# Four of 22 row pieces of the indexer's sum on GpSimd in place of VectorE

## What is computed

```python
isc = jax.nn.relu(jnp.einsum('bqhd,bsd->bqhs', qib, k_idx).astype(jnp.float32))
isc = jnp.einsum('bqh,bqhs->bqs', wib.astype(jnp.float32), isc) * idx_scale
isc = jnp.where(admissible[None], isc, -jnp.inf)
top_val, top_idx = lax.top_k(isc, top_k)
```

## Time and profile before

| | us |
|---|---|
| median of 3 runs | 3939.31 (3933.16 to 3941.74) |
| profiled execution, its own time | 3942.32 |
| its span, first to last instruction | 3940.5 |
| VectorE's additions of the indexer, L2115 and L2118 | from 1899.96 to the end of the stage |

### The profile page before, as it was taken

How to read it: one execution, slowest core, us unless ns; L and a number is a source line. 1 busy time by engine, 2 the same in 40 slices (tenths; PEclk the granted TensorE clock), 3 DMA queues, 4 the chain that set the end, 5 groups by cost and what they waited for, 6 DMA issues and landing times. The chain is left out here.

```text
span 3940.5 us, 83555 instructions
## 1 busy us (share of the span) xinstructions
PE 3586.9 (91%) x32524; PEld 3086.8 (78%) x32524; DVE 2307.3 (59%) x5832; ACT 2064.4 (52%) x4636; POOL 766.7 (19%) x657
## 2 busy tenths in 40 slices
PE   5999999889899989979679989976899999999899
PEld 4777899878687768867557987965688888888687
DVE  6100110057898973320699989977677777777322
ACT  4222111156788862212677657554577777777311
POOL 3222100012666640002005425314100000000000
PEclk9999999989999999989899999988899999999899
DMA  5333321196442323452313354235744443341432
GB/s 192 108 117 112 122 81 49 52 204 156 98 97 64 79 74 132 142 197 98 87 43 123 117 168 139 92 135 197 170 96 90 98 92 87 85 97 45 148 122 79
DMA packets 332879, 441.66 MB, mean 112 GB/s; under 512 B 17608, under 2 KB 254792, under 8 KB 322760
## 3 DMA queue, kind: packets, MB, share of 16 engines
q1 hardware_dynamic: 250328, 318.54, 30.6%
q10 hardware_dynamic: 82176, 117.98, 8.1%
HBM read 272.37 MB, written 164.10 MB: 111 GB/s over the span
## 5 line engine op out<-in xcount | busy, mean ns | idle before, releaser
L1265 PEld LDWEIGHTS s_o<-s_v,s_pT 128*64 128x64 f32 x13056 | 402.2, 138 | 89.7 <-issue 68.9
L1265 PE MATMUL s_o<-s_v,s_pT 128*64 128x64 f32 x13056 | 436.9, 224 | 20.3 <-issue 20.3
L211 PE MATMUL s_acc<-s_wh,s_hT 128*128 128x256 f32 (+1 forms) x1408 | 430.5, 306 | 7.1 <-ACT s_parts L624 3.1
L212 PE MATMUL s_acc<-s_wl,s_hT 128*128 128x256 f32 (+1 forms) x1408 | 429.4, 305 | 0.0
L213 PE MATMUL s_acc<-s_wh,s_hT 128*128 128x256 f32 (+1 forms) x1408 | 429.1, 305 | 0.0
L1418 ACT ACTIVATE s_probs<-s_probs,s_nmx 128x512 f32<-128x512 f32 (+3 forms) x640 | 417.0, 657 | 11.7 <-DVE s_nmx L1464 11.7
L211 PE MATMUL s_acc<-s_hT,s_wh 128*128 128x512 f32 x880 | 351.4, 399 | 67.4 <-DVE s_wl L310 29.7
L1250 PE MATMUL s_s<-s_kh,s_qs 128*128 128x512 f32 (+3 forms) x944 | 376.1, 402 | 32.5 <-ACT s_pos L2099 12.3
L1453 DVE CUSTOM_DVE_ANT_0 s_probs<-s_s,s_scores 128x512 f32<-128x512 f32 (+3 forms) x640 | 371.3, 607 | 7.8 <-PEq L91 7.6
L2191 DVE TENSOR_SCALAR_CACHE_REDUCE s_scratch<-s_scores,s_thr 128x384 uint8<-128x384 f32 (+4 forms) x320 | 365.3, 1209 | 1.1
L212 PE MATMUL s_acc<-s_hT,s_wh 128*128 128x512 f32 x880 | 348.6, 396 | 0.0
(11 more groups left out here) (248 smaller groups left out, 7751.1 us busy)
## 6 DMA issues: line engine op xcount, KB each, us to landing
fm<-s_parts ACTq DMA_DIRECT2D x120, 512.0 KB, 2.8
s_qs<-fm SPq DMA_DIRECT2D x60, 512.0 KB, 6.5
y<-s_g SPq DMA_DIRECT2D x20, 1024.0 KB, 5.1
s_y<-y SPq DMA_DIRECT2D x32, 640.0 KB, 6.1
kc<-s_parts ACTq DMA_DIRECT2D x32, 512.0 KB, 2.9
s_kh<-kc SPq DMA_DIRECT2D x30, 512.0 KB, 10.3
s_kl<-kc SPq DMA_DIRECT2D x30, 512.0 KB, 11.9
s_w<-in_o_fm SPq DMA_DIRECT2D x25, 512.0 KB, 4.7
```

Source lines behind the costliest of these rows:

```text
L211: nc.tensor.matmul(out, sh, mh, start=(j == 0), stop=False)
L212: nc.tensor.matmul(out, sh, ml, start=False, stop=False)
L1265: last = nc.tensor.matmul(o_ps[r:r + HD, 0:HD], pT[:, x * P + r:x * P + r + HD], v[:, g.u.kbs[g.a + x], vc:vc + HD], start=(g.first and x ...
```

## The change

Of each head's 22 pieces four, (4,0) of 640 columns, (10,8) of 384, (12,8) of 640 and (14,8) of 896, go to GpSimd. In head 0 GpSimd multiplies such a piece into the sums by one `tensor_scalar`. In heads 1 to 7 it takes two instructions: `tensor_scalar` weighs the piece in place in `pos`, and, behind a wait for that one (`weighed`), `tensor_tensor` adds it to the sums. `added` is now two semaphores, one for each adder, and ScalarE waits for the one of the engine that holds the buffer. TensorE's and ScalarE's work, the order of the units and the rings stay.

```diff
+    BY_POOL = ((4, 0), (10, PB), (12, PB), (14, PB))
     units = [(h, b, a, m) for h in range(I_HEADS) for b, a, m in pieces]
+    adder = ["p" if (b, a) in BY_POOL else "v" for _, b, a, _ in units]
+    nth = [adder[:ui + 1].count(adder[ui]) for ui in range(len(units))]
...
-        added = sc.sem("added")
+        added = {"v": sc.sem("added_v"), "p": sc.sem("added_p")}
+        weighed = sc.sem("weighed")
...
                     if ui >= 4:
-                        act.wait_ge(added, ui - 3)
+                        act.wait_ge(added[adder[ui - 4]], nth[ui - 4])
...
                 for ui, (h, b, a, m) in enumerate(units):
+                    if adder[ui] == "p":
+                        continue
...
                     else:
-                        dve.wait_ge(added, ui - per_head + 1)
+                        dve.wait_ge(added["v"], nth[ui - per_head])
...
+            @block.gpsimd
+            def _(pool):
+                pool.wait_ge(w_made, 1)
+                for ui, (h, b, a, m) in enumerate(units):
+                    if adder[ui] == "v":
+                        continue
+                    dst, src = scores(b)[:, a * P:(a + m) * P], pos[ui % 4][:, 0:m * P]
+                    pool.wait_ge(clipped, ui + 1)
+                    if h == 0:
+                        nc.gpsimd.tensor_scalar(dst, src, w[:, b, h:h + 1], None, ALU.mult).then_inc(added["p"], 1)
+                    else:
+                        pool.wait_ge(added["p"], nth[ui - per_head])
+                        nc.gpsimd.tensor_scalar(src, src, w[:, b, h:h + 1], None, ALU.mult).then_inc(weighed, 1)
+                        pool.wait_ge(weighed, nth[ui] - len(BY_POOL))
+                        nc.gpsimd.tensor_tensor(dst, dst, src, ALU.add).then_inc(added["p"], 1)
```

More of the change, by code:

```diff
@@ L2114, in _ @@
                     if h == 0:
-                        nc.vector.tensor_scalar(dst, src, w[:, b, h:h + 1], None, ALU.mult).then_inc(added, 1)
+                        nc.vector.tensor_scalar(dst, src, w[:, b, h:h + 1], None, ALU.mult).then_inc(added["v"], 1)
                     else:
-                        dve.wait_ge(added, ui - per_head + 1)
+                        dve.wait_ge(added["v"], nth[ui - per_head])
                         nc.vector.scalar_tensor_tensor(out=dst, in0=src, scalar=w[:, b, h:h + 1], in1=dst,
-                                                       op0=ALU.mult, op1=ALU.add).then_inc(added, 1)
+                                                       op0=ALU.mult, op1=ALU.add).then_inc(added["v"], 1)
+            @block.gpsimd
[13 more added lines that the diff above has]
+                        nc.gpsimd.tensor_tensor(dst, dst, src, ALU.add).then_inc(added["p"], 1)
 class Search:
```

## The result

| | median | runs |
|---|---|---|
| before | 3939.4 us | 4, 3933.2 to 3941.7 |
| changed | 3967.6 us | 4, 3965.6 to 3968.2 |

The ratio is 1.0081 (1.0069 to 1.0094): 28 us by the medians, 32 by the ratio, 27 to 37 by its interval. The prediction said 3968, range 3953 to 3988, slower.

The account below looks back on a forecast made before the run. VectorE was taken to bound heads 1 to 7 at 20.6 us each. GpSimd's holds of 7.35 us less 3.2 saved gave +4.1 a head, 28.9 on 3939.3, so 3968 us, range 3953 to 3988.

Parts of the forecast that it names:

- The bound: In heads 1 to 7 VectorE sets the pace, 20.6 us a head without idle time; the other engines wait for it.
- What is taken: Four pieces' additions leave VectorE in each of heads 1 to 7, 3.2 us a head; VectorE alone would need 17.4.
- `tensor_tensor`, 6.24 us a head: GpSimd's four additions in each of heads 1 to 7, at 2.18 ns a column and 0.165 us fixed.
- `tensor_scalar`, 2.87 us a head at the `CAST`'s rate: GpSimd's four weighings in each of heads 1 to 7, at 0.84 ns a column and 0.18 us fixed; upper bound 6.24.
- Turns, one instruction at a time, whichever came first goes first: VectorE and GpSimd alternate when both read SBUF; each GpSimd instruction costs VectorE its duration less some 0.22 us.
- The holds, 7.35 us a head: Time GpSimd's eight instructions keep VectorE waiting in each of heads 1 to 7: 9.11 us less 1.8.
- The ring, 0 to 14 us, taken as 0: ScalarE waiting for buffers of GpSimd's slower pieces: at most 0.5 us for each of 28 pieces, expected just in time.
- The sum, +28.9: 7.35 us of holds against 3.2 saved, net +4.1 a head, 28.9 us for seven heads; head 0 adds 0.
- 1 (no hold): GpSimd and VectorE don't get in each other's way; a head at 18.7 us, 13 us less, 3926; chance 0.08.
- 2 (dearer): Holds plus dearer `tensor_scalar` (24 us) or ring turns (up to 14): 3987 with half of both, 4006 in full; chance 0.17.
- 3: The hold just eats the saving, with half the hold that the trace shows; 3937 to 3945 us; chance 0.07.
- 4 (clock): TensorE's clock falls in the stage, 37 us more, 4005; sign a granted clock below 0.9 there; chance 0.04.

Follow-up runs that it names:

- psum_pool: GpSimd has its four pieces as in the changed kernel, but VectorE's 18 pieces are clipped in place and read in PSUM; 1.0004 of the kernel before.
- tiny: The changed kernel with GpSimd's two instructions of heads 1 to 7 cut to one column; 0.9971 of the kernel before.
- only_add: The changed kernel without GpSimd's weighing in heads 1 to 7, leaving only its `tensor_tensor`; 1.0040 of the kernel before.
- own_buffers: The changed kernel with two SBUF buffers of GpSimd's own for its pieces, outside VectorE's ring of four; 3967.2 us, 1.0086 of the kernel before.
- the probe: The kernel before plus stretches timing GpSimd's instructions alone and beside VectorE; 896-column `tensor_tensor` held VectorE 1.81 us with SBUF inputs, nothing with one in PSUM.
- the second timing: The changed kernel itself timed again with more rounds, beside the kernel before on another chip; 3971.1 against 3936.9 us, ratio 1.0083.

## Why the prediction was right, step by step

- **The bound** (VectorE, 20.6 us a head, no slack): right. What was put on it and taken from it showed in the stage's length, except where idle time covered it.
- **What is taken, 3.2 us a head**: right; psum_pool's 126 additions, unheld, are busy for 125.2 us, and tiny's for 123.0, against the 121.7 that the subtraction gives; where there are gaps, fewer records overlap.
- **`tensor_tensor`, 6.24 us a head**: right to 2%; alone 0.99 + 2 x 1.53 + 2.07 = 6.1 us.
- **`tensor_scalar`, 2.87 us a head at the `CAST`'s rate**: wrong as a duration. It is 1.24 + 2 x 1.885 + 2.53 = 7.5 us, 2.50 ns a column, above even the upper bound of 6.24, the two-input rate. Right as a hold, by luck: the 0.75 us that it holds happen to be what a `CAST` takes. The nearest row gave the right number for another reason than the prediction had. The best of a loop in the Trainium skill ("GPSIMD Engine Reference", section "Performance versus the Vector engine"), 1.8 cycles an element or 1.5 ns a column, is not reached; the measured 2.50 decides.
- **Turns, one instruction at a time, whichever came first goes first**: right for the prices, wrong as a rule. GpSimd's weighing of (10,8) in the changed kernel, 1.24 us alone, has a mean of 2.41: it lets a VectorE instruction go first that began after it. In tiny and only_add it lets four go first, 4.66 and 5.38 us.
- **The holds, 7.35 us a head**: right where VectorE never idles (7.3 in own_buffers), 6.0 in the changed kernel, because idle time covers some.
- **The ring, 0 to 14 us, taken as 0**: this term was mis-sized: 13.5 us. The time until the buffer of (14,8) is free was right, 5.5 us reckoned and 5.4 measured from the end of its clip (1986.97 to 1992.36). Wrong was that VectorE has four additions to do meanwhile. Three pieces can be clipped behind (14,8), that is three additions, (15,0), (15,8) and (2,0), done at 1992.78; the fourth, (3,0), needs this very buffer, and then (5,0) comes late too: 0.85 us a head. The other 0.88 are the same wait for the buffer of (12,8), which the prediction did not look at.
- **The end**: GpSimd's last piece ends 1.9 us after VectorE's. The prediction did not look at it. Head 0 costs 0.9 us, within its "0, at most 1".
- **The sum, +28.9**: the stage gained 36 us, 33 in the seven heads. 42.2 + 13.5 - 22.4 = 33.3 against 51.4 - 22.4 = 29. The terms' errors partly cancel, fewer holds against more idle time. The total of 28 in the first timing is nearer to the sum than the stage is, and that is chance, as is a median within 0.4 us of the 3968; the second timing gave 34.
- **The rivals**: 1 (no hold) is out by the probe and psum_pool. 2 (dearer) was in part true: the ring cost 13.5 us, while the dearer rate of `tensor_scalar` showed in its duration and not in its hold. 3 is out. 4 (clock): the clock was 0.82 to 0.98 in the heads, below the 0.9 that the prediction named as a sign, but for short spells only; at 0.90 the heads kept their 25.5 us, and at 0.83 they were up to 0.9 us longer, 1 to 2 us in all in place of 37.

Not settled: why `tensor_scalar` lasts three times as long as it holds, and why GpSimd is sometimes passed over by several VectorE instructions; no kernel took either apart.

## What to carry to other kernels

Before moving elementwise work from VectorE to GpSimd, look at what VectorE reads: with two inputs in SBUF, a GpSimd instruction that reads SBUF can take from VectorE more than it saves (here 3.2 us saved, 7.3 lost a head, of which the four `tensor_scalar` are only some 2); with one of them in PSUM it takes nothing, but the banks are then held longer, and a plain multiplication from PSUM is slower. Look for a place in the trace where the same pair of instructions already runs side by side, and read both durations against those alone, for each kind of instruction that moves: a duration on GpSimd is not yet the hold. And a slower engine in a shared ring costs by its latency, even if its share of the time is small: count its pieces' waits before its work.

## What the runs showed of the hardware that was not expected

- GpSimd's `tensor_scalar` with a per-partition scalar is slower than its `tensor_tensor`: 2.53 against 2.07 us for 896 columns, 2.50 and 2.10 ns a column.
- It holds VectorE for only 0.75 of those 2.53 us (896 columns).
- A GpSimd instruction beside a busy VectorE can be passed over again and again: one column took 0.28 us without VectorE, mostly 1.05 beside it, and 4.66 once a head in tiny; 384 columns took 5.38 in only_add, 0.99 alone.
- A `scalar_tensor_tensor` is no slower from PSUM than from SBUF: 1.275 against 1.280 us for 1024 columns. A `tensor_scalar` is: 1.278 against 0.753.
